# Feed-forward by groups of six weight units: down products beside gate and up products

## The reference

```
swiglu(x, w_gate, w_up, w_down) = (silu(x @ w_gate) * (x @ w_up)) @ w_down
x = x + 0.5 * swiglu(rmsnorm(x, n_f1), f1_g, f1_u, f1_d)
x = x + mixers(rmsnorm(x, n_mix))        # short convolution and gated delta rule
x = x + 0.5 * swiglu(rmsnorm(x, n_f2), f2_g, f2_u, f2_d)
y = rmsnorm(x, norm_final)
```

## Time and profile before

| what | value |
|---|---|
| time, median of 2 runs | 3886.61 us (3886.1 to 3887.11) |
| span of the profiled execution, first to last instruction | 3881.5 us |
| PE busy | 3496.9 us, 90% |
| DVE, ACT, POOL busy | 30%, 23%, 23% |
| PE matmuls of the two feed-forwards | 9504 of 21156 rows |
| mean granted TensorE clock | 0.952 |
| DMA | 213.92 MB, 55 GB/s over the span |

### The profile page before, as it was taken

One profiled execution on the slowest core, in us unless ns is written; L12 is line 12 of the kernel. 1 busy time (PEld: TensorE's weight loads), 2 busy tenths in 40 slices (PEclk: granted clock), 3 DMA queues, 4 the chain that ended last, 5 costly groups with the idle time before them and its releaser, 6 DMA issues. The chain is left out here.

```text
span 3881.5 us, 54022 instructions
## 1 busy us (share of the span) xinstructions
PE 3496.9 (90%) x21156; PEld 3389.9 (87%) x21156; DVE 1149.3 (30%) x1951; ACT 891.7 (23%) x1420; POOL 901.3 (23%) x518
## 2 busy tenths in 40 slices
PE   6999899997999999999598888868897999999997
PEld 6999899996999999999487777858897999999996
DVE  3222222224222555100333444422323222222224
ACT  3111111112111333322234333321122111111112
POOL 2111211113122112122243344311132111111113
PEclk8999999998999999999799999979998999999998
DMA  2111111110112223232101111013411111111111
GB/s 87 42 44 39 44 39 34 44 44 22 50 53 62 84 84 95 90 96 79 59 19 42 65 42 59 24 60 118 127 46 38 44 38 43 38 43 32 43 43 46
DMA packets 238735, 213.92 MB, mean 55 GB/s; under 512 B 7050, under 2 KB 214026, under 8 KB 238576
## 3 DMA queue, kind: packets, MB, share of 16 engines
q1 hardware_dynamic: 238276, 211.51, 17.7%
q10 hardware_dynamic: 324, 0.41, 0.0%
HBM read 166.13 MB, written 45.76 MB: 55 GB/s over the span
## 5 line engine op out<-in xcount | busy, mean ns | idle before, releaser
L158 PE MATMUL ffn_bank<-ffn_h_hi,ffn_w_hi 128*128 128x368 f32 x2112 | 699.8, 331 | 46.5 <-DVE ffn_h_lo L533 37.9
L159 PE MATMUL ffn_bank<-ffn_h_lo,ffn_w_hi 128*128 128x368 f32 x2112 | 699.3, 331 | 0.0
L160 PE MATMUL ffn_bank<-ffn_h_hi,ffn_w_lo 128*128 128x368 f32 x2112 | 697.8, 330 | 0.0
L144 POOL TENSOR_TENSOR ffn_w_lo<-ffn_w_raw,ffn_w_hi 128x1024 fp32r<-128x1024 f32 x132 | 314.2, 2380 | 1434.1 <-ACT ffn_w_hi L139 1433.8
L158 PE MATMUL inp_bank<-inp_h_hi,inp_w_hi 128*128 128x368 f32 x1752 | 580.5, 331 | 29.0 <-DVE inp_h_lo L827 25.5
L159 PE MATMUL inp_bank<-inp_h_lo,inp_w_hi 128*128 128x368 f32 x1752 | 580.0, 331 | 0.0
L160 PE MATMUL inp_bank<-inp_h_hi,inp_w_lo 128*128 128x368 f32 x1752 | 578.8, 330 | 0.0
L158 PE MATMUL ffn_bank<-ffn_mid_hi,ffn_w_hi 128*128 128x368 f32 x1056 | 370.0, 350 | 98.2 <-POOL ffn_w_lo L144 98.2
L158 PEld LDWEIGHTS ffn_bank<-ffn_h_hi,ffn_w_hi 128*128 128x128 f32 x2112 | 398.4, 189 | 52.1 <-issue 38.4
L160 PEld LDWEIGHTS ffn_bank<-ffn_h_hi,ffn_w_lo 128*128 128x128 f32 x2112 | 398.1, 188 | 0.0
L159 PEld LDWEIGHTS ffn_bank<-ffn_h_lo,ffn_w_hi 128*128 128x128 f32 x2112 | 397.8, 188 | 0.0
(11 more groups left out here) (251 smaller groups left out, 4543.8 us busy)
## 6 DMA issues: line engine op xcount, KB each, us to landing
inp_w_raw<-in_w_in SPq DMA_DIRECT2D x73, 512.0 KB, 4.1
ffn_w_raw<-in_ffn_w_gate SPq DMA_DIRECT2D x44, 512.0 KB, 3.9
ffn_w_raw<-in_ffn_w_up SPq DMA_DIRECT2D x44, 512.0 KB, 3.9
ffn_w_raw<-in_ffn_w_down SPq DMA_DIRECT2D x44, 512.0 KB, 3.6
scratch_qkv<-inp_out SPq DMA_DIRECT2D x24, 552.0 KB, 2.8
scratch_y_a<-inp_out SPq DMA_DIRECT2D x8, 552.0 KB, 3.2
scratch_z<-inp_out SPq DMA_DIRECT2D x8, 552.0 KB, 5.2
scratch_sig_a<-inp_out SPq DMA_DIRECT2D x8, 552.0 KB, 3.4
```

The lines of the kernel that those rows point to most:

```text
L144: pool.tensor_tensor(self.lo[:, k, :, :], self.raw[:, k, :, :], self.hi[:, k, :, :].bitcast(F32), ALU.subtract).then_inc(self.lo_done, 1)
L158: pe.matmul(out, w_hi, x_hi, start=first, stop=False)
L159: pe.matmul(out, w_hi, x_lo, start=False, stop=False)
L160: return pe.matmul(out, w_lo, x_hi, start=False, stop=last)
```

## The change

`WeightStream` is replaced in `ffn` by `GroupStream`: three raw slots, and six hi and lo slots, one for each unit of a group (0 to 3 gate and up, 4 and 5 down). A load waits for the lo split of the unit three before it; a hi split waits for the product that read the slot one group earlier (`gu_done`, or `down_done` at the head of `group`). PE no longer sends `split_free`. PE's order becomes gate and up of group g, then down of group g; at its first chunk the down waits for `mid_ready` third by third. `mid_hi` and `mid_lo` lose their second buffer. The loop holds one group and turns ten times. ACT splits units 2 and 3 of the first group right after the copies of `h`, and units 4 and 5 of each group ahead of its silus. In the last group the down products go third by third, the squares use two buffers, each add waits for the add before it, and each sum over partitions is issued when its third is done, in a bank of its own; the sums of the second and third thirds wait for the Ln of the one before. In the cut below a line of dots stands for removed or unchanged lines.

```diff
@@ -329,6 +329,23 @@
         part = third(n % NB)
         pool.tensor_tensor(self.rstd[:, part], self.rstd[:, part], self.sq[:, part], ALU.add).then_inc(self.added, 1)
 
+    def square_part(self, act, x_part, b, c):
+
+        act.wait_ge(self.added, NB + max(KC * b + c - 1, 0))
+        act.activation(self.sq[:, c % 2, third(b)], x_part, ACT.Square).then_inc(self.squared, 1)
+
+    def add_part(self, pool, b, c):
+        pool.wait_ge(self.squared, KC * b + c + 1)
+        part = third(b)
+        pool.wait_ge(self.added, NB + KC * b + c)
+        pool.tensor_tensor(self.rstd[:, part], self.rstd[:, part], self.sq[:, c % 2, part], ALU.add).then_inc(self.added, 1)
+
+    def sum_part(self, pe, out, b):
+        pe.wait_ge(self.added, NB + KC * (b + 1))
+        if b:
+            pe.wait_ge(self.logged, b)
+        pe.matmul(out, self.ones, self.rstd[:, third(b)], start=True, stop=True).then_inc(self.summed, 1)
+
     def sum(self, pe, out, b):
         pe.wait_ge(self.added, NB * KC + b + 1)
         pe.matmul(out, self.ones, self.rstd[:, third(b)], start=True, stop=True).then_inc(self.summed, 1)
@@ -342,88 +359,149 @@
             act.activation(self.rstd[:, third(b)], self.rstd[:, third(b)], ACT.Exp, scale=-0.5).then_inc(self.factor, 1)
 
 
+class GroupStream:
+    RAW, UNITS = 3, 6
+    def __init__(self, s):
+        self.raw = s.sb("w_raw", [P, self.RAW, KC, P])
+        self.hi = s.sb("w_hi", [P, self.UNITS, KC, P], F32R)
+        self.lo = s.sb("w_lo", [P, self.UNITS, KC, P], F32R)
+        self.raw_loaded = [s.sem(f"w_raw_loaded{k}") for k in range(self.RAW)]
+        self.hi_done = s.sem("w_hi_done")
+        self.lo_done = s.sem("w_lo_done")
+    def load(self, sp, i, g, u, src, rows=False):
+        n = self.UNITS * g + u
+        if n >= self.RAW:
+            sp.wait_ge(self.lo_done, i * self.UNITS + (n - self.RAW + 1))
+        dst = self.raw[:, u % self.RAW, :, :]
+        sp.dma_start(dst, src).then_inc(self.raw_loaded[u % self.RAW], 16)
+    def split_hi(self, act, i, g, u):
+        per = self.UNITS // self.RAW
+        act.wait_ge(self.raw_loaded[u % self.RAW], i * (16 * per) + 16 * (per * g + u // self.RAW + 1))
+        act.activation(self.hi[:, u, :, :], self.raw[:, u % self.RAW, :, :], ACT.Copy).then_inc(self.hi_done, 1)
+    def split_lo(self, pool, i, g, u):
+        pool.wait_ge(self.hi_done, i * self.UNITS + (self.UNITS * g + u + 1))
+        pool.tensor_tensor(self.lo[:, u, :, :], self.raw[:, u % self.RAW, :, :], self.hi[:, u, :, :].bitcast(F32),
+                           ALU.subtract).then_inc(self.lo_done, 1)
+    def wait(self, pe, i, g, u):
+        pe.wait_ge(self.lo_done, i * self.UNITS + (self.UNITS * g + u + 1))
 def ffn(nc, name, x, rstd, gains, g_at, ones, eps_col, w_gate, w_up, w_down):
...
     GROUPS = FF // (2 * P)
...
+    GU, DN, USES = 12, 24, 6
...
+        mid_hi = s.sb("mid_hi", [P, 2, T], F32R)
+        mid_lo = s.sb("mid_lo", [P, 2, T], F32R)
+        w = GroupStream(s)
...
+        sum_bank = s.ps("sum_bank", [P, 512])
+        nrm = NextNorm(s, rstd, ones, eps_col, hid)
...
+        def last_order():
+            return [(c, b) for b in range(NB) for c in range(KC)]
         @block.sync
         def _(sp):
...
+            def gate_up(i, g):
                 for a in range(2):
...
+                    w.load(sp, i, g, 2 * a, gate_src(i, g, a))
+                    w.load(sp, i, g, 2 * a + 1, up_src(i, g, a))
+            def down(i, g):
                 for a in range(2):
...
+                    w.load(sp, i, g, 4 + a, down_src(i, g, a))
             gate_up(0, 0)
...
+            with sp.Fori(0, GROUPS - 1) as i:
+                down(i, 0)
+                gate_up(i, 1)
+            down(0, GROUPS - 1)
         @block.gpsimd
         def _(pool):
...
+            for u in range(4):
+                w.split_lo(pool, 0, 0, u)
+            with pool.Fori(0, GROUPS - 1) as i:
+                for u in (4, 5):
+                    w.split_lo(pool, i, 0, u)
+                for u in range(4):
+                    w.split_lo(pool, i, 1, u)
+            for u in (4, 5):
+                w.split_lo(pool, 0, GROUPS - 1, u)
             pool.wait_ge(h_ready, KC)
             nrm.clear(pool)
...
+            for b in range(NB):
+                for c in range(KC):
+                    nrm.add_part(pool, b, c)
         @block.tensor
         def _(pe):
...
             for k in range(6):
                 pe.sem_inc(bank_free[k], 1)
...
+            def bank_wait(i, g, k6, use):
+                pe.wait_ge(bank_free[k6], i * USES + (USES * g + use + 1))
+            def gate_up_unit(i, g, u):
+                a, q = divmod(u, 2)
+                w.wait(pe, i, g, u)
+                for b in range(NB):
+                    k6 = 3 * q + b
+                    bank_wait(i, g, k6, a)
+                    for k in range(KC):
+                        mm = three_passes(pe, bank[k6][:, 0:TH], w.hi[:, u, k, :], w.lo[:, u, k, :],
+                                          h_hi[:, k, third(b)], h_lo[:, k, third(b)], k == 0, k == KC - 1)
+                    mm.then_inc(gu_done, 1)
+            def down_part(i, g, c, b, n):
+                k6 = n % 6
+                bank_wait(i, g, k6, 2 + n // 6)
+                for a in range(2):
+                    mm = three_passes(pe, bank[k6][:, 0:TH], w.hi[:, 4 + a, c, :], w.lo[:, 4 + a, c, :],
+                                      mid_hi[:, a, third(b)], mid_lo[:, a, third(b)], a == 0, a == 1)
+                mm.then_inc(down_done, 1)
+            def down(i, g):
+                w.wait(pe, i, g, 5)
+                for c in range(KC):
+                    for b in range(NB):
+                        if c == 0:
+                            pe.wait_ge(mid_ready, i * 6 + (6 * g + 3 + b + 1))
+                        down_part(i, g, c, b, NB * c + b)
+            w.wait(pe, 0, 0, 1)
...
+            for u in (2, 3):
+                gate_up_unit(0, 0, u)
+            with pe.Fori(0, GROUPS - 1) as i:
+                down(i, 0)
+                for u in range(4):
+                    gate_up_unit(i, 1, u)
+            w.wait(pe, 0, GROUPS - 1, 5)
+            for n, (c, b) in enumerate(last_order()):
+                if c == 0:
+                    pe.wait_ge(mid_ready, 6 * (GROUPS - 1) + 3 + b + 1)
+                down_part(0, GROUPS - 1, c, b, n)
+                if b and c == KC - 1:
+                    nrm.sum_part(pe, sum_bank[:, 0:TH], b - 1)
+            nrm.sum_part(pe, sum_bank[:, 0:TH], NB - 1)
         @block.scalar
         def _(act):
...
+            for u in range(2):
+                w.split_hi(act, 0, 0, u)
             for k in range(KC):
                 act.wait_ge(h_scaled, k + 1)
                 act.copy(h_hi[:, k, :], hid[:, k % 2, :]).then_inc(h_hi_done, 1)
...
+            for u in (2, 3):
+                w.split_hi(act, 0, 0, u)
+            def next_split(i, g, u):
+                act.wait_ge(gu_done, i * GU + (GU * g + 3 * u + 3))
+                w.split_hi(act, i, g + 1, u)
+            def group(i, g, ahead):
+                if g or not isinstance(i, int):
+                    act.wait_ge(down_done, i * DN + DN * g)
+                for u in (4, 5):
+                    w.split_hi(act, i, g, u)
                 for a in range(2):
...
                     for b in range(NB):
...
+                        act.wait_ge(gu_done, i * GU + (GU * g + 6 * a + b + 1))
                         act.activation(hid[:, a, third(b)], bank[b][:, 0:TH], ACT.Silu).then_inc(bank_free[b], 1)
...
+                    if ahead:
+                        next_split(i, g, 2 * a)
                     for b in range(NB):
...
+                        act.wait_ge(bank_free[3 + b], i * USES + (USES * g + a + 2))
+                        act.copy(mid_hi[:, a, third(b)], hid[:, a, third(b)]).then_inc(mid_hi_done, 1)
+                    if ahead:
+                        next_split(i, g, 2 * a + 1)
+            act.wait_ge(h_ready, KC)
+            group(0, 0, True)
+            with act.Fori(0, GROUPS - 2) as i:
+                group(i, 1, True)
+            group(0, GROUPS - 1, False)
+            act.wait_ge(mid_ready, 6 * GROUPS)
+            for b in range(NB):
+                for c in range(KC):
+                    act.wait_ge(x_final, KC * b + c + 1)
+                    nrm.square_part(act, x[:, c, third(b)], b, c)
+            nrm.factors(act, lambda b: sum_bank[:, 0:TH])
         @block.vector
         def _(dve):
@@ -533,39 +579,32 @@
                 dve.tensor_tensor(h_lo[:, k, :], hid[:, k % 2, :], h_hi[:, k, :].bitcast(F32),
                                   ALU.subtract).then_inc(h_ready, 1)
...
+            def gate_up(i, g):
                 for a in range(2):
                     for b in range(NB):
...
+                        dve.wait_ge(gu_done, i * GU + (GU * g + 6 * a + 3 + b + 1))
+                        dve.wait_ge(bank_free[b], i * USES + (USES * g + a + 2))
```

(60 more changed lines are left out.)

52 lines of the change are left out of this document (1 added, 51 removed).

## The result

The changed kernel takes **3753.9 us** (median of two runs, 3749.5 and 3758.3) against 3886.6 us: a ratio of 0.966, 95% interval 0.963 to 0.969, 3.4% faster. The forecast was 3752 us, the range 3735 to 3775. The profiled execution's span is 3747.3 us; it took 3749.5 us in all, so 2.2 us lie around its first and last instruction. For the kernel before that is 1.8 us as well (3887.4 us against a span of 3885.6 in one of its later runs), so the 5.1 us given above are not all of that kind: by these rows some 3.3 us of them are an execution, the profiled one, that was shorter than the median.

A forecast was written before the change was run, and what follows sets the result against it. TensorE was taken to bound the kernel, busy 90% of the span. 3881.5 - 152.0 + 2.2 + 5.7 + 4.0 + 6 gave a span of 3747.4 us, with 5.1 us around it 3752 us; range 3735 to 3775.

The forecast's parts named there:

- the 5.1 us: Time around the span, added to the forecast span of 3747.4 us to give 3752 us.
- Down starts and turns: Both feed-forwards' bodies: 152.0 us of lost TensorE time come back, first feed-forward's loop turns included; 2.2 us of bubbles added.
- the restarts after the third unit: After the third-unit gap in each feed-forward: TensorE restarts at the lower clock, 2.0 us each, +4.0 us.
- The 0.1 us bubbles: At each of 22 down starts, waiting for the last third's mid_lo: 0.1 us each, +2.2 us (0 to 4.4).
- Loop turns at nothing: PE's loop branch, taken 18 times in place of 8, costed at nothing, as under already queued matmuls.
- The rival with code at the turns: PE stops 1.0 us at each of 18 loop turns: 3770 us in place of 3752; chance 12%.
- Third unit, +5.7 and +4.0: Start of each feed-forward: PE waits 5.9 us against 3.05 for ACT's silu, +5.7; lower-clock restarts, +4.0.
- Ends, +6 (0 to 10): End of each feed-forward: chained Ln and sums and tied adds cost +3 us each, +6 together (0 to 10).
- The adds: Feed-forward ends: POOL's adds each wait for the one before; up to 0.14 us lag over 23 adds, 3.3 us late.
- The chain: Feed-forward ends: three Ln and two sums in turn take 3.6 us against 1.49 before, +2.1 us.
- The late third: Down starts: late mid_lo makes a 1.9 us PE gap and lower-clock restart, 86 us over 22: 3838 us; chance 5%.
- The raw ring: Each group: a late unit 5 load holds ACT's silus, 11 us in each of 20 groups: 3972 us; chance 2%.

## Why the prediction was right

In total it was right to 2 us, in its steps less so: one size was off, and a stage that the change does not touch covered for it. That it came so close was luck; the two runs behind the median lie 8.8 us apart themselves.

- **Down starts and turns, 152.0 us back, less 2.2.** Right. The bodies gave 145.2 us. Two things that are not of this term lie in them: the restarts after the third unit, costed apart (2.5 and 1.8 us), and the first sum over partitions, about 0.6 us in each (with the silus moved, bodies of 774.1 us with it and 773.5 without). That makes 150.7 us, against 149.8 forecast. The 0.1 us bubbles did not show: the first down matmul starts 0.17 us after the last up matmul, the thirteenth in its slot. That the wait was ACT's order is shown by the moved split alone; that the thirds hide a chain of 2 us, by the exposed one.
- **Loop turns at nothing.** Right, and shown with the longer body. The rival with code at the turns (12%) fell.
- **Third unit, +5.7 and +4.0.** Right in mechanism and size: heads +2.8 and +3.0, restarts about 2.5 and 1.8. Moving the silus took both away.
- **Ends, +6 (0 to 10).** The step that failed in size: 6.9 and 5.8, 12.7 together, outside its bounds. Two terms of it were too small. The adds: I took 0.9 us of lag at each end; in the first feed-forward the last square comes 2.5 us later than before (3.4 against 0.9 us after the last down matmul), in the second 2.1. Tied, the adds run at 1.1 us in place of 1.0; my limit of 0.14 us over 23 adds, which is 3.2 us and not 3.3, was the nearer figure, and 0.9 had no row behind it. The chain: I took 2.1 more; from the first Ln's start to the last one's end it is 5.2 us against 1.5, so 3.7. I had priced the sums by a row at full clock, 0.86 us; here PE had been idle 5.6 us, the granted clock is 0.50, and each takes 1.56. Undoing the end shows the two together, adding a bank shows a turn of the chain. The 0.7 us that are left of the first end's 6.9 come in the next stage, and their cause is open.
- **What covered it.** The delta-rule stage was 7.5 us shorter in the profiled execution than in the one before (739.5 against 747.0 us); run again it was 3.2 longer. With the ends sized right the sum would have been about 3759, which is what the later runs of the changed kernel gave (3758.1). The 5.1 us that the sum adds stand for the difference between the profiled execution and the median of before, not for time around the span; as a step from one to the other they do no harm.
- **The other rivals.** The late third (5%): `mid_lo` was in time at every down start. The raw ring (2%): the hi splits at the head of a group never held a bank up inside the loop; the same mechanism at the first group was the third unit's 5.9 us.

## What to carry to other kernels

When the busiest engine waits for an operand that is made late, look first at what stands ahead of that operand in its maker's queue: one moved split was worth as much here as six slots and a new order. (With its third unit and its ends mended, the new order is 26 us ahead of that split: 3725.4 against 3751.5 us.) When such a change shortens the middle, cost its two ends with the same care, since queues are filled and emptied there in another order; and price an instruction that follows idle time at the lower clock.

## What the runs showed of the hardware that was not expected

- A gap of 2.25 us before the same 144 matmuls lowered the granted clock in 6 of 20 cases and left it at 2.4 GHz in 14; gaps of 4.86 us, in the kernel before, lowered it in all 20.
- The delta-rule stage, with the same code, took between 739.5 and 751.2 us in the ten executions that were traced; in the shortest its granted clock was 0.92, in the other nine 0.90 or 0.91, whether they took 743 or 751 us, so the clock alone does not tell them apart; the cause is open. Between the two traces of the changed kernel it makes 10.8 of the 10.9 us by which their spans differ. It is larger than several of the effects measured here, so stages had to be compared and not totals.
- The same loop body of 864 matmuls takes its branch at 3.5 us in the first feed-forward and at 0.2 us in the second, in the kernel before and in the changed kernel with two groups in a turn.
